# One-hots of each token with the gate in the same VectorE instruction, and a third buffer for the high parts of the first expert matrix

## What is computed

```python
s = jnp.einsum('thjd,jkd->thjk', qry, keys)          # 8 heads, two halves, 128 keys each
s_top, i_top = lax.top_k(s, 16)
cand = s_top[:, :, 0, :, None] + s_top[:, :, 1, None, :]
best, pos = lax.top_k(cand.reshape(..., 256), 16)    # 16 of 16384 experts for each head
gates = jax.nn.softmax(best, axis=-1)
act = gelu(einsum('thkd,td->thk', peer_u[idx], x))
y = einsum('thk,thkd->td', gates * act, peer_v[idx])
```

## Time and profile before

| | us |
|---|---|
| median of 3 runs | 2455.06 |
| the runs | 2452.28 to 2457.01 |
| the profiled execution, time | 2455.18 |
| its span, first to last instruction | 2453.4 |
| TensorE busy in the span | 2307.6 (94%) |
| VectorE busy | 1534.7 (63%) |
| ScalarE busy | 893.1 (36%) |
| GpSimd busy | 1130.3 (46%) |

### The profile page before, as it was taken

How to read it: one execution, slowest core, us unless ns; L and a number is a source line. 1 busy time by engine, 2 the same in 40 slices (tenths; PEclk the granted TensorE clock), 3 DMA queues, 4 the chain that set the end, 5 groups by cost and what they waited for, 6 DMA issues and landing times.

```text
span 2453.4 us, 33207 instructions
## 1 busy us (share of the span) xinstructions
PE 2307.6 (94%) x12935; PEld 1958.8 (80%) x12935; DVE 1534.7 (63%) x2567; ACT 893.1 (36%) x1175; POOL 1130.3 (46%) x554
## 2 busy tenths in 40 slices
PE   6999999959888999999999999999999999999998
PEld 4998899747648987787778878888788888888886
DVE  4766579455722167887899887775555555555552
ACT  3434455561222133323345444455332232222221
POOL 0333246154623246556655765455554444444441
PEclk8999999988998999999999999999999999999999
DMA  7221122647654345555547886686665554455440
GB/s 269 69 87 54 57 72 69 187 139 221 192 189 121 83 121 143 129 154 130 136 131 183 246 249 191 170 216 184 237 229 205 191 202 178 182 204 205 188 154 35
DMA packets 307405, 392.67 MB, mean 160 GB/s; under 512 B 14545, under 2 KB 257637, under 8 KB 302914
## 3 DMA queue, kind: packets, MB, share of 16 engines
q1 hardware_dynamic: 212162, 302.86, 40.5%
q10 hardware_dynamic: 91664, 75.54, 9.5%
q0 software_dynamic: 3456, 12.58, 1.6%
HBM read 305.70 MB, written 81.26 MB: 158 GB/s over the span
## 4 chain that ended last, share of the span: by engine, by line
PE 56%; DVE 4%; POOL 3%; DMA 2%; ACT 1%; issue 1%; ACTq 0%; DVEq 0%
PE bank L2589 28%; PE bank L2046 22%; PE bank L2540 3%; DVE work L2266 2%; POOL utL_hid L2036 2%; DMA work<-sample_rows_dram 1%; DVE work L2269 1%; PE bank L2545 1%; DVE ut_hid L2025 1%; PE bank L2527 1%; POOL work L2224 0%; DVE work L2339 0%; ACT utH_hid L2032 0%; DMA work<-in_peer_u_dram,eu_sm 0%; POOL work L1967 0%
## 5 line engine op out<-in xcount | busy, mean ns | idle before, releaser
L2036 POOL TENSOR_TENSOR utL_hid<-ut_hid,utH_hid 128x1024 fp32r<-128x1024 f32 x128 | 348.0, 2719 | 329.5 <-ACT utH_hid L2032 328.9
L2046 PE MATMUL bank<-pH,utH_hid 128*128 128x512 f32 x1024 | 407.0, 397 | 13.4 <-POOL utL_hid L2036 13.4
L2046 PE MATMUL bank<-pH,utL_hid 128*128 128x512 f32 x1024 | 399.7, 390 | 0.0
L2046 PE MATMUL bank<-pL,utH_hid 128*128 128x512 f32 x1024 | 399.6, 390 | 0.0
L2589 PE MATMUL bank<-area,work 128*128 128x512 f32 x1536 | 350.8, 389 | 0.0
L2589 PEld LDWEIGHTS bank<-area,work 128*128 128x128 f32 x1536 | 288.3, 188 | 59.9
L2025 DVE STREAM_TRANSPOSE ut_hid<-u_hid 128x1024 f32<-128x1024 f32 x128 | 158.8, 1241 | 146.8 <-POOL utL_hid L2036 127.1
L2202 POOL TENSOR_TENSOR pL<-work,pH 128x1024 fp32r<-128x1024 f32 x64 | 155.1, 2423 | 193.8 <-ACT pH L2445 193.7
L824 POOL TENSOR_TENSOR wL_in<-wb_in,wH_in 128x1024 fp32r<-128x1024 f32 x52 | 129.4, 2488 | 243.7 <-ACT wH_in L777 243.7
L864 PE MATMUL ps_in<-hH_in,wH_in 128*128 128x260 f32 x816 | 238.2, 292 | 2.4 <-DVE projarea L915 1.4
L2046 PEld LDWEIGHTS bank<-pH,utH_hid 128*128 128x128 f32 x1024 | 193.0, 188 | 56.5 <-POOL utL_hid L2036 18.7
(11 more groups left out here) (533 smaller groups left out, 4457.8 us busy)
## 6 DMA issues: line engine op xcount, KB each, us to landing
u_hid<-in_peer_u_dram SPq DMA_DIRECT2D x256, 256.0 KB, 5.0
work<-in_peer_v_dram SPq DMA_DIRECT2D x64, 1024.0 KB, 4.9
hidden_dram<-ge_hid ACTq DMA_DIRECT2D x64, 512.0 KB, 3.1
gates_dram<-area ACTq DMA_DIRECT2D x16, 2048.0 KB, 10.3
wb_in<-in_w_in_dram SPq DMA_DIRECT2D x26, 1024.0 KB, 5.3
wstage<-in_w_ada_dram SPq DMA_DIRECT2D x32, 512.0 KB, 4.9
area<-hidden_dram SPq DMA_DIRECT2D x16, 1024.0 KB, 6.8
area<-gates_dram SPq DMA_DIRECT2D x16, 1024.0 KB, 8.7
```

The source lines that it names most:

```text
L2036: self.nc.gpsimd.tensor_tensor(self.utL[:, u % 2], self.ut[:, u % 2], self.utH[:, u % 2].bitcast(F32), ALU.subtract).then_inc(self.low, 1)
L2046: mm = self.nc.tensor.matmul(self.pa[u % 2][:, :], w[:, u % 2, k, :], x[:, k, :], start=(n == 0), stop=(n == 3 * KD - 1))
```

## The change

The diff does five things.

- `utH` has three buffers. `move_high(u)` waits for `hide(u-3)` where it waited for `hide(u-2)`. `move_low(u)` now waits for `hide(u-2)` itself, as `utL` keeps its two buffers.
- ScalarE runs one unit further ahead: `move_high(1)` stands among the evictions before the units, and iteration u does `move_high(u+2)`.
- VectorE runs one turn further ahead: `turn(2)` stands before the loop and iteration u begins with `turn(u+3)`. `ut` keeps its two buffers, and `turn` its wait.
- `one_hots(q)` makes eight instructions of 128 columns: for each of four tokens the row's compare with the multiplication by the gate in the same instruction, and the column's compare. The rows, columns and gates are read as one scalar per partition.
- GpSimd's multiplications go, and with them the semaphores of the compare and of both multiplications; one semaphore, `hot`, tells TensorE that a quad is ready.

```diff
--- before.py
+++ after.py
@@ -2001,7 +2001,7 @@
         self.u = [sb(f"u{i}", [P, 2 * 4, D // 4]) for i in range(2)]
         self.ge = [sb(f"ge{i}", [P, 2, T]) for i in range(2)]
         self.ut = sb("ut", [P, 2, KD, P])
-        self.utH = sb("utH", [P, 2, KD, P], F32R)
+        self.utH = sb("utH", [P, 3, KD, P], F32R)
         self.utL = sb("utL", [P, 2, KD, P], F32R)
         self.uv = A["peer_u"][0].rearrange("(g r) (a f) -> a r g f", r=32, a=4)
         self.u_in = [ctx.sem(f"u_in{i}") for i in range(2)]
@@ -2027,13 +2027,15 @@
 
     def move_high(self, act, u):
         act.wait_ge(self.turned, u + 1)
-        if u >= 2:
-            act.wait_ge(self.hidden, u - 1)
-        self.nc.scalar.activation(self.utH[:, u % 2], self.ut[:, u % 2], ACT.Copy).then_inc(self.high, 1)
+        if u >= 3:
+            act.wait_ge(self.hidden, u - 2)
+        self.nc.scalar.activation(self.utH[:, u % 3], self.ut[:, u % 2], ACT.Copy).then_inc(self.high, 1)
 
     def move_low(self, pool, u):
         pool.wait_ge(self.high, u + 1)
-        self.nc.gpsimd.tensor_tensor(self.utL[:, u % 2], self.ut[:, u % 2], self.utH[:, u % 2].bitcast(F32), ALU.subtract).then_inc(self.low, 1)
+        if u >= 2:
+            pool.wait_ge(self.hidden, u - 1)
+        self.nc.gpsimd.tensor_tensor(self.utL[:, u % 2], self.ut[:, u % 2], self.utH[:, u % 3].bitcast(F32), ALU.subtract).then_inc(self.low, 1)
 
     def hide(self, pe, u):
 
@@ -2042,8 +2044,8 @@
             pe.wait_ge(self.gelued, u - 1)
         n = 0
         for k in range(KD):
-            for w, x in ((self.utH, self.S.pH), (self.utH, self.S.pL), (self.utL, self.S.pH)):
-                mm = self.nc.tensor.matmul(self.pa[u % 2][:, :], w[:, u % 2, k, :], x[:, k, :], start=(n == 0), stop=(n == 3 * KD - 1))
+            for w, x in ((self.utH[:, u % 3], self.S.pH), (self.utH[:, u % 3], self.S.pL), (self.utL[:, u % 2], self.S.pH)):
+                mm = self.nc.tensor.matmul(self.pa[u % 2][:, :], w[:, k, :], x[:, k, :], start=(n == 0), stop=(n == 3 * KD - 1))
                 n += 1
         mm.then_inc(self.hidden, 1)
 
@@ -2119,12 +2121,12 @@
         vL = [carve(work, 8192, (P, JG, D), F32R), flat(S.pL).rearrange("p (a b) -> p a b", b=D)]
         ab = [carve(sc, 0, (P, JG, T)), flat(H.u[0]).rearrange("p (a b) -> p a b", b=T)]
         gb = [carve(sc, 2048, (P, NTB, JG, TB)), flat(H.u[1]).rearrange("p (a b c) -> p a b c", b=JG, c=TB)]
-        wH = [carve(sc, 4096, (P, JG, T), F32R), H.utH[:, :, :, :].rearrange("p a k n -> p (a k n)").rearrange("p (a b) -> p a b", b=T)]
+        wH = [carve(sc, 4096, (P, JG, T), F32R), H.utH[:, 0:2, :, :].rearrange("p a k n -> p (a k n)").rearrange("p (a b) -> p a b", b=T)]
         wL = [carve(sc, 6144, (P, JG, T), F32R), H.utL[:, :, :, :].rearrange("p a k n -> p (a k n)").rearrange("p (a b) -> p a b", b=T)]
 
         keys_in, keys_t, keys_s, gathered, scored, kept = (sem(n + "_sc") for n in ("keys_in", "keys_t", "keys_s", "gathered", "scored", "kept"))
         m = {n: sem(n + "_ex") for n in ("own", "shifted", "gates", "picked", "hit", "res", "res_t", "res_s", "s_shifted", "s_gates", "s_res", "s_moved",
-                                         "compared", "hot_dve", "hot_pool", "multiplied", "staged", "stored0", "stored1",
+                                         "lowered", "hot", "multiplied", "staged", "stored0", "stored1",
                                          "numbered", "us_in0", "us_in1", "xs_in0", "xs_in1", "dotted", "gelued_s", "weighed_s", "vs_in", "mixed_s", "accs")}
         v_in, a_in, g_in = ([sem(f"{n}_in{i}_v") for i in range(2)] for n in "vag")
         v_high, v_low, weighted, w_high, w_low, mixed = (sem(n + "_v") for n in ("high", "low", "weighted", "w_high", "w_low", "mixed"))
@@ -2218,10 +2220,6 @@
                     picked = K.pick(nc.gpsimd, 4 + r)
                     if r == 1:
                         picked.then_inc(m["picked"], 1)
-                for q in QUADS[u]:
-                    if q % 2:
-                        pool.wait_ge(m["compared"], q + 1)
-                        nc.gpsimd.tensor_tensor(oh[q % OH][:, 0], oh[q % OH][:, 0], bcast(S.sel[:, 2, 4 * q:4 * q + 4], 2, P), ALU.mult).then_inc(m["hot_pool"], 1)
                 if u == 80:
                     pool.wait_ge(m["numbered"], 1)
                     gather_u(0)
@@ -2254,7 +2252,6 @@
         def _(dve):
             V = nc.vector
             own = Chain(dve, m["own"])
-            iota4 = bcast(bcast(S.iota[:, :], 1, 4), 1, 2)
             dve.sem_inc(w_low, 2 * JG)
 
             def one_hots(q):
@@ -2263,10 +2260,11 @@
                     dve.wait_ge(m["multiplied"], q - OH + 1)
                 if q % (L // 4) == 0:
                     dve.wait_ge(m["res_s"], q // (L // 4) + 1)
-                V.tensor_tensor(o, iota4, bcast(S.sel[:, 0:2, 4 * q:4 * q + 4], 3, P), ALU.is_equal).then_inc(m["compared"], 1)
-                if q % 2 == 0:
-                    dve.wait_ge(m["compared"], q + 1)
-                    V.tensor_tensor(o[:, 0], o[:, 0], bcast(S.sel[:, 2, 4 * q:4 * q + 4], 2, P), ALU.mult).then_inc(m["hot_dve"], 1)
+                for t in range(4):
+                    of = lambda n: S.sel[:, n, 4 * q + t:4 * q + t + 1]
+                    V.tensor_scalar(o[:, 0, t, :], S.iota[:, :], of(0), of(2), ALU.is_equal, ALU.mult)
+                    last = V.tensor_scalar(o[:, 1, t, :], S.iota[:, :], of(1), None, ALU.is_equal)
+                last.then_inc(m["hot"], 1)
 
             def select(i, r):
 
@@ -2377,9 +2375,10 @@
             H.turn(dve, 0)
             H.turn(dve, 1)
             dve.wait_ge(kept, 17)
+            H.turn(dve, 2)
             for u in range(UNITS):
-                if u + 2 < UNITS:
-                    H.turn(dve, u + 2)
+                if u + 3 < UNITS:
+                    H.turn(dve, u + 3)
                 i, r = divmod(u, PER_TILE)
                 if 1 <= i <= NC:
                     number(i - 1, r)
@@ -2424,8 +2423,8 @@
             for n in range(16):
                 act.wait_ge(scored, n + 2)
                 nc.scalar.activation(S.sc[:, n // 4, 4 * (n % 4):4 * (n % 4) + 4, :], quad[n % 4], ACT.Copy).then_inc(kept, 1)
-                if n == 11:
-                    H.move_high(act, 0)
+                if n in (11, 13):
+                    H.move_high(act, (n - 11) // 2)
 
             def evict(q):
                 b, blk = q // PER_BLOCK % 2, q // PER_BLOCK
@@ -2450,8 +2449,8 @@
 
             ends = Chain(act, e["act_own"])
             for u in range(UNITS):
-                if u + 1 < UNITS:
-                    H.move_high(act, u + 1)
+                if u + 2 < UNITS:
+                    H.move_high(act, u + 2)
                 if u:
                     for q in QUADS[u - 1]:
                         evict(q)
@@ -2528,10 +2527,7 @@
                     mm.then_inc(scored, 1)
 
             def place(q):
-                if q % 2:
-                    pe.wait_ge(m["hot_pool"], q // 2 + 1)
-                else:
-                    pe.wait_ge(m["hot_dve"], q // 2 + 1)
+                pe.wait_ge(m["hot"], q + 1)
                 if q >= 4:
                     pe.wait_ge(m["staged"], q - 3)
                 else:
```

## The result

The changed kernel takes 2502.91 us (median; 2499.38 to 2509.03), the kernel before, run beside it, 2456.03. The ratio is 1.0192 (95% interval 1.0163 to 1.0221): slower by some 47 us where +30 was forecast. The direction and the range held; the size did not.

A forecast was written before the change was run, and what follows sets the result against it. TensorE's chain was taken to bound the kernel, losing 42 us among the units; changes by stretch (-1, +12.7, 0, +11.6, -6.3, +12.8, last unchanged) summed to +29.8 on 2455.2, forecasting 2485 us, range 2448 to 2524.

The forecast's parts named there:

- Part 1, the gate: VectorE's iteration u: turn(u+3) and all behind it wait for low(u+1), so the first one-hot starts at E + 3.77.
- E: The end of hide(u-1), from which the prediction counts the queues of iteration u.
- Part 2, the one-hots: VectorE's eight TENSOR_SCALARs a quad: 1.76 us, from 0.24 with two scalars and 0.20 with one.
- Rival A: One-hots at most 1.19 us a quad, so three quads fit before the low; faster, 2449 or 2443 us; chance 0.18.
- Part 3, the port: GpSimd's low gets between VectorE's one-hots and stops one for 2.41 us; a three-quad unit loses 2.4 us.
- rival C: Overlapped TENSOR_SCALARs keep the port, so GpSimd doesn't get in; about the same, +4, 2459 us; chance 0.15.
- Rival B: Two quads don't fit before the low either; 1.6 us lost in some 25 two-quad units; +40, 2525 us; chance 0.15.
- Units 91 to 121: Six three-quad units lose 2.4 us each, 14.4, where 1.6 was lost before: +12.8 us.
- Units 62 to 67: Reductions in iterations 64 and 66 cost 4.2 us each, picks before unit 62's one-hot 9: +12.7 us.
- Units 74 to 83: Three-quad units 75, 79 and 83 lose 7.2 us, gathers ahead of low(82) 4.4: together +11.6 us.
- Units 68 to 73 and 84 to 90: First stretch counted 0; second loses 7.6 us in units 85, 87, 89 where 13.9 was lost: -6.3 us.
- Units 0 to 61: Wait for the high gone, but low, find and pick queue for one port; bounds 12 gained and nothing, 1 taken.

The follow-up runs named there:

- low_after: Changed kernel, but GpSimd makes the low part of unit u+1 only after VectorE's one-hots of unit u-1 are done; 2470.30 us, ratio 1.0067.
- turn_2: Changed kernel, but VectorE turns unit u+2 in its iteration, as the kernel before does, not unit u+3; 2439.54 us, ratio 0.9940.
- oh_first: Changed kernel, but VectorE does the selection and one-hots of unit u ahead of turn(u+3); 2440.55 us, ratio 0.9940.
- buf_only: Kernel before with only the third buffer and the moved turns and highs, one-hots made as before; 2508.24 us, ratio 1.0203.

## Why the prediction was right in direction and short in size

*Part 1, the gate: right.* The queue from E was forecast with the first one-hot at E + 3.77, two quads done at 7.29, the next low ready at 7.34 and the third quad's end at 11.5; unit 111 shows 3.96, 7.54, 7.55 and 11.58. The first three are 0.2 late because a low starts 0.31 behind its hide, not 0.1. Of the signs, the turn within 0.1 of the low's end was to be seen in nearly every unit from 68 on; it is in 40 of the iterations 68 to 121, and ten of the other 14 follow a unit with three quads.

*Part 2, the one-hots: right.* A quad takes 1.77 to 1.81 (1661.15 to 1662.92 to 1664.73), forecast 1.76; with two scalars an instruction is followed after 0.25, with one after 0.20, as the earlier trace rows gave it. Rival A, which needed 1.19, falls. The estimate of 1.0 us a quad from the Trainium skill, VectorE: DVE Perf Modes (section on the TRN2 errata), falls with it: the trace disagrees, 1.77.

*Part 3, the port: right.* GpSimd gets in between two overlapped TENSOR_SCALARs, one stretches to 2.48 beside a low of 2.39, and rival C falls. The Trainium skill, SBUF — State Buffer (section Who interferes with whom), speaks of a lock that is held by an instruction; the trace agrees in that the stop is as long as the low. The recorded starts don't tell who gets in: the stopped one-hot starts 0.01 before the low. Rival B was near, though: the low is ready 0.01 behind the start of the third quad, and two quads just fit.

*Units 91 to 121: the term right, another missing.* Units 91, 99, 107, 115 and 119 lose 2.7, 2.7, 2.7, 1.8 and 2.7 more than before; 111 loses 2.7, of which 1.3 stood there before. That is 14.2 more against the 12.8 of the sum. The other 4.9 are the hides of units 92, 100 and 112, 1.62 longer each. The chain of the changed kernel has the hides of units 108 and 112 as follows (start us, us, what):

```profile
1635.56 5.49 PE bank L2048 x24
...
1669.98 7.09 PE bank L2048 x24
```

Windows of the changed kernel, from the end of the hide of 91 to the start of the hide of 92, and that hide:

```profile
1487.23:1492.55 5.32, 2.86 (x25) 2.66 (x24) 5.32 (x11) 1.58 (x3) 2.41 (x1) 1.00 1.12 330
1492.55:1499.71 7.16, 7.16 (x27) 5.77 (x26) 3.85 (x18) 2.98 (x4) 0.00 (x0) 0.76 0.98 267
```

In the window with the 2.46 us wait the granted clock is 1.00, in the hide behind it 0.76: part of it at the lower of the two levels, 1.2 GHz, the rest at 2.4. The prediction took a wait on TensorE as its own length and had no term for this; this is the step that fell short. The sign had stood in the kernel before, in the clock of 0.95 in units 84 to 90: there, after a wait of 2.01, a place of unit 89 and the hide of 90 are as slow (start us, us, what):

```profile
1440.47 2.07 PE bank L2540 x8
1442.55 7.47 PE bank L2046 x24
```

In `low_after`, whose longest wait there is 0.7, hides 92, 100 and 112 are at their usual length. No run holds the clock by itself: that the waits lower it is read from this and from the order in time.

*Units 62 to 67: the same missing term, and one pick.* VectorE, GpSimd and TensorE's places in unit 64 and 65 of the changed kernel:

```profile
1239.40 1.25 DVE L2025 STREAM_TRANSPOSE ut_hid<-u_hid 128x1024 f32<-128x1024 f32 x1 [9.08 <-POOL utL_hid L2038]
1240.57 3.44 DVE L1983 TENSOR_REDUCE work<-work 128x64 f32<-128x3200 f32 x1
1244.05 1.70 DVE L2265 TENSOR_SCALAR work<-iota,sel 128x128 f32<-128x128 f32 x1
1245.68 1.77 DVE L2266 TENSOR_SCALAR work<-iota,sel 128x128 f32<-128x128 f32 x1
...
1243.32 2.35 POOL L2038 TENSOR_TENSOR utL_hid<-ut_hid,utH_hid 128x1024 fp32r<-128x1024 f32 x1 [2.23 <-PE bank L2048]
1245.63 1.73 POOL L1967 TENSOR_TENSOR work<-work,work 128x800 f32<-128x800 f32 x1
...
1248.86 2.08 PE L2536 MATMUL bank<-work 128*128 128x128 f32 x8 [5.68 <-DVE work L2266]
1257.66 1.05 PE L2536 MATMUL bank<-work 128*128 128x128 f32 x8
```

After a wait of 5.68 the place of unit 64 takes 2.08, where one behind a wait of 2.44 took 1.16 in unit 111 above; the next hide starts 0.8 later for it. So it is in 62 and 66. The hides behind them (63, 65, 67) last 7.50, 7.07 and 7.52 instead of 5.54. That makes 2.5 + 5.5, about 8 of the 21.0, and the 0.81 in the windows' clock; the 13 that are left stand against a forecast of 12.7. In it unit 66 loses, without its slow place, 4.4 (4.2 forecast); unit 64 5.9, because GpSimd's pick (1.73) follows the low and stops a second one-hot, which I had not put into that queue; and unit 62 7.5 where 9 was forecast. The prediction's queue for unit 62 counts from the end of hide 58, though it says E(59), as find(0) stands in iteration 59. Counted from there (1197.03), the one-hots are done and TensorE's place starts at 30.4, forecast 31.8.

*Units 74 to 83.* The three-quad units 75, 79 and 83 lose 3.5, 2.2 and 3.4 more than before (7.2 forecast, 9.1 measured), unit 81 behind the gathers 4.9 (4.4 forecast), and the hide of 76 is 0.8 longer. Units 75 and 83 pay 0.8 more than 107 because here the clock falls already in the place; unit 75's and the hide of 76 in the chain (start us, us, what):

```profile
1349.43 2.07 PE bank L2536 x8
1351.51 6.14 PE bank L2048 x24
```

The two places of unit 81 take 3.5 instead of 1.7 by their starts, so 1.8 of its 4.9 are clock too. Clock makes 4.2 of the stretch's 14.9; the 10.7 that are left stand against the 11.6.

*Units 68 to 73 and 84 to 90.* The +2.6 in 68 to 73 are less than what the clock takes there: 2.1 in longer hides (69 and 72) and 1.2 in places of 68 and 71. In 84 to 90, -6.6 stands against -6.3, in part by luck: units 85, 87 and 89 were to lose 7.6, but 86 and 89 lose 4.9 by late one-hots, and the hides of 84 and 87 2.4 by clock.

*Units 0 to 61: the wrong end of the bounds.* The bounds were 12 gained and nothing; I took 1, because low, find and pick still queue for one port. Measured are 7.1. The kernels with three buffers that hold no gate in front of VectorE gain all of it: units 0 to 61 take 338.7 in `turn_2` and in `oh_first`, 343.6 in the changed kernel and in `buf_only`, 350.7 before. The wait for the high was what cost; the port takes nothing, and the gate gives 5 back.

Summed, from the forecast's +29.8 to the 49.3 between the spans: about 20 are the missing clock term (8 + 3.3 + 4.2 + 2.4 + 4.9 = 22.8, less 2.9 that the kernel before loses so in units 89 and 90), -6 the early units, 5 lie ahead of unit 0, and within 1 us nothing is left over. That the early units and the start cancel is luck.

*TensorE's waits before: misread.* The prediction calls the 13.4 us for the low TensorE's longest wait. The longest, in total and singly, is that of places for GpSimd's multiplication (same query as the earlier trace rows):

```profile
PE bank L2540 <- POOL work L2224: 15.4, 14, 2.1
```

The sum doesn't rest on it, since the losses were taken from the lengths of stretches.

What stays open: TensorE waits 2.46 us in unit 107 as in unit 91, and yet the hide behind it, that of 108, keeps its length (5.49 above); so do those of 116 and 120. The runs don't tell which waits lower the clock.

## What to carry to other kernels

When a buffer lets one engine run ahead, look at what else is moved with it: a wait that comes one unit earlier in an in-order queue delays everything behind it. Here the buffer is a gain with the turn left in place and a loss with it moved. And a stop of one engine by another costs nothing while the stopped one is ahead; judge such a collision by the slack of the engine that is stopped, not by its length.

## What the runs showed of the hardware that was not expected

A wait of TensorE may cost more than its length: after waits of 2.0 to 7.2 us the next work ran partly at the lower clock (behind a wait, a place 2.08 instead of 1.16; a hide 7.09 instead of 5.49, granted clock 0.76 in such a one), which added 1.6 to 2.9 us to some of the waits and nothing to others of 2.46. And GpSimd's instruction gets in between VectorE's inside a row of overlapped TENSOR_SCALARs. In the changed kernel 18 one-hots are stopped, ten of them the first of their eight and eight a later one; GpSimd's instruction starts from 0.7 us before the stopped one to 0.08 after it, and the stopped one ends 0.08 or 0.09 behind GpSimd's.
